# Attention turns: VectorE's copy of the transposed weights issued first in its turn

## The reference, cut to what matters

```python
s_lat = jnp.einsum('bnqhgd,bnkhd->bhgnqk', qb, kb).astype(jnp.float32) * scale
s_lat = jnp.where(valid, s_lat, -jnp.inf)
...
p = jax.nn.softmax(jnp.concatenate([s_lat, s_ctx, s_sink], axis=-1), axis=-1).astype(v.dtype)
out = (jnp.einsum('bhgnqk,bnkhd->bnqhgd', p[..., :nk], vb)
       + jnp.einsum('bhgnqc,bchd->bnqhgd', p[..., nk:nk + nc], vc))
```

## Time and profile before

| | |
|---|---|
| median of 3 runs | 1475.39 us (1473.77 to 1479.74) |
| the profiled execution | 1478.54 us, span of its trace 1476.7 us |
| PE busy | 1359.0 us, 92% of the span |
| DVE busy | 1039.2 us, 70% |
| ACT, POOL busy | 643.8 us, 225.9 us |
| granted TensorE clock, mean | 0.947 of full |
| L995, the copy | 40 times, 526 to 692 ns |
| first pass, in the span | 127.4 to 217.6 us |
| layer 3's pass | 1194.6 to 1230.1 us |

### The profile page before, as it was taken

The page is one execution under the profiler, slowest core; times in us unless marked ns, Lnnn a source line. Parts: engine busy times, 40 slices in busy tenths (PEclk is TensorE's granted clock), DMA queues, the critical chain, the costliest instruction groups (busy, mean ns, idle before and its releaser), DMA issues. The chain is left out here.

```text
span 1476.7 us, 24608 instructions
## 1 busy us (share of the span) xinstructions
PE 1359.0 (92%) x9014; PEld 1177.8 (80%) x9014; DVE 1039.2 (70%) x1803; ACT 643.8 (44%) x1287; POOL 225.9 (15%) x294
## 2 busy tenths in 40 slices
PE   6898999499999999979999999999999978899977
PEld 4576678388888888868896789999899967899857
DVE  0698867889697796988416675766664975755964
ACT  2424761242231423325226654455455465455563
POOL 2030221100000000012102710000210126010324
PEclk7898999699999999989999999999999989899988
DMA  7954124357578575744220155665465533445511
GB/s 279 274 172 156 55 62 143 128 185 268 188 243 284 194 264 179 253 175 143 87 90 25 30 157 171 213 185 185 132 222 171 162 96 107 144 144 170 173 42 44
DMA packets 67799, 236.14 MB, mean 160 GB/s; under 512 B 7296, under 2 KB 12416, under 8 KB 67456
## 3 DMA queue, kind: packets, MB, share of 16 engines
q1 hardware_dynamic: 67712, 234.98, 48.7%
HBM read 233.90 MB, written 1.05 MB: 159 GB/s over the span
## 5 line engine op out<-in xcount | busy, mean ns | idle before, releaser
L768 DVE TENSOR_TENSOR wlo<-raw,whi 128x1024 fp32r<-128x1024 f32 x286 | 361.8, 1267 | 176.4 <-ACT whi L501 171.9
L501 ACT ACTIVATE whi<-raw 128x1024 fp32r<-128x1024 f32 x286 | 301.6, 1055 | 244.3 <-PE ps L1353 232.4
L1351 PE MATMUL ps<-Hh,whi 128*128 128x512 f32 (+1 forms) x848 | 297.2, 351 | 17.3 <-DVE Hl L885 14.2
L1352 PE MATMUL ps<-Hl,whi 128*128 128x512 f32 (+1 forms) x848 | 295.1, 348 | 0.0
L1353 PE MATMUL ps<-Hh,wlo 128*128 128x512 f32 (+1 forms) x848 | 295.0, 348 | 0.0
L1351 PEld LDWEIGHTS ps<-Hh,whi 128*128 128x128 f32 x848 | 162.9, 192 | 41.7 <-issue 14.8
L1351 PE MATMUL ps<-Gh,whi 128*128 128x256 f32 x624 | 180.5, 289 | 4.5 <-DVE Gl L885 3.8
L1352 PEld LDWEIGHTS ps<-Hl,whi 128*128 128x128 f32 x848 | 163.1, 192 | 21.4
L1353 PEld LDWEIGHTS ps<-Hh,wlo 128*128 128x128 f32 x848 | 162.7, 192 | 21.8
L1352 PE MATMUL ps<-Gl,whi 128*128 128x256 f32 x624 | 179.0, 287 | 0.0
L1353 PE MATMUL ps<-Gh,wlo 128*128 128x256 f32 x624 | 178.7, 286 | 0.0
(11 more groups left out here) (212 smaller groups left out, 2110.9 us busy)
## 6 DMA issues: line engine op xcount, KB each, us to landing
raw<-wall SPq DMA_DIRECT2D x286, 512.0 KB, 4.3
aring<-aall SPq DMA_DIRECT2D x144, 512.0 KB, 4.4
AL<-ali SPq DMA_DIRECT2D x14, 192.0 KB, 5.4
X<-xin SPq DMA_DIRECT2D x1, 2048.0 KB, 11.7
BI<-rpb SPq DMA_DIRECT2D x4, 512.0 KB, 16.6
cst<-const SPq DMA_DIRECT2D x1, 1216.0 KB, 11.4
out<-X SPq DMA_DIRECT2D x4, 256.0 KB, 2.5
par<-prm SPq DMA_DIRECT2D x1, 134.5 KB, 2.2
```

The lines of the kernel that those rows point to most:

```text
L501: act.activation(whi[:, slot, :], raw[:, slot, :], ACT.Copy).then_inc(sem("w_hi"), 1)
L768: dve.tensor_tensor(wlo[:, slot, :], raw[:, slot, :], whi[:, slot, :].bitcast(F32), ALU.subtract)\
L1351: pe.matmul(o, a[0], b[0], start=first, stop=False)
L1352: pe.matmul(o, a[0], b[1], start=False, stop=False)
```

## The change

VectorE's copy of head 1's transposed weights of job s-2 is put at the head of its turn, ahead of bias and maximum of job s. Its waits go with it. Nothing is added or removed; no other engine's program changes.

```diff
             def attend(j0, j1):
                 for s in range(j0, j1 + 4):
+                    if j0 <= s - 2 < j1 and not jobs[s - 2].diff:
+
+                        g = s - 2
+                        dve.wait_ge(sem("t_done"), g + 1)
+                        if g >= 2:
+                            dve.wait_ge(sem("pv_done"), g - 1)
+                        dve.tensor_copy(PT[:, g % 2, 1, 0:jobs[g].nk], ps[:, 5, 0:jobs[g].nk]).then_inc(sem("ev_v"), 1)
                     if s < j1:
...
                             dve.scalar_tensor_tensor(e0, e1, st[:, 12:13], e0, ALU.mult, ALU.add)\
                                .then_inc(sem("normed"), 1)
-                    if j0 <= s - 2 < j1 and not jobs[s - 2].diff:
-
-                        g = s - 2
-                        dve.wait_ge(sem("t_done"), g + 1)
-                        if g >= 2:
-                            dve.wait_ge(sem("pv_done"), g - 1)
-                        dve.tensor_copy(PT[:, g % 2, 1, 0:jobs[g].nk], ps[:, 5, 0:jobs[g].nk]).then_inc(sem("ev_v"), 1)
                     if j0 <= s - 4 < j1 and jobs[s - 4].diff:
```

## The result

The changed kernel takes 1485.57 us (median of 4 runs, 1483.78 to 1487.89) against 1475.55 us for the kernel before on the same chip (4 runs, 1473.77 to 1479.74). The ratio is 1.0069, 95% interval 1.0049 to 1.0089: 10.0 us slower, where 8.6 were forecast. The profiled execution took 1486.57 us with a span of 1484.8. The mean granted clock is 0.947 of full in both profiles.

A forecast was written before the change was run, and what follows sets the result against it. It took a VectorE-GpSimd ring to bound layers 3 and 4, and TensorE the first pass. Gated passes 7.0 plus first pass 1.6 gave 8.6 us over 1475.4, so 1484.0 us, with 8 in 10 between 1478.5 and 1488.

The forecast's parts named there:

- The gain: TensorE's 10 waits for the copy, 6.6 us, are all there is to win; six end without moving anything.
- The full turns: Layers 3 and 4: the copy adds 0.44 to each turn, 3.62 to 4.06 us; three distances, 1.32 us a pass.
- the ring: Layers 3 and 4: bias, maximum, reciprocal, GpSimd's widening and gate, product, next bias; this loop sets the turn at 3.62 us.
- The first turns: Layers 3 and 4: the copy waits for the first transposes and delays bias and maximum; first product 2.10 us later.
- The first pass: Stalls of 0.3 us after turns 5, 8 and 11, 0.4 at the end, 0.3 for the fill: 1.6 us.
- the fill: Start of the first pass, not worked out by row: 0.3 us taken, between no loss and 2.1.
- idle until L1501 in each of 24 turns: First pass, sign in the timeline: VectorE's copy waits for TensorE's transposes in every one of 24 turns.
- the clock: Layers 3 and 4: TensorE busy about 3.1 of 4.06 us keeps full clock, so the sum has no term for it.
- The rival made of it: Clock falls to half rate in the longer gaps of layers 3 and 4: +13 us, 1496.5; chance 0.05.
- the softer bound: Layers 3 and 4 less tightly bound, half the loss regained, first pass losing next to nothing: 1479.5 us; chance 0.2.
- the faster case: Every wait for the copy lies on the path that sets the end: -6.6 us, 1468.8; chance 0.04.
- the latency ring in the first pass: Copy, bias, maximum, exponentials and scores follow one another; 24 turns each 0.15 later, 3.6 us more: 1487.5; chance 0.1.

The follow-up runs named there:

- the first pass alone: Against the kernel before, the copy moved to the head of the turn only in the first pass: 1476.76 us against 1477.32, ratio 0.9999.

## Why the prediction was right

**The gain.** That the waits for the copy would go and bring nothing: right. 6.6 us of waits went, the time rose.

**The full turns.** Forecast 4.06, measured 4.08 in each of six distances; the copy holds back by 0.46, not 0.44. The wait for the gate became 1.18, forecast 1.1 to 1.2. That the place sets the price is shown by the kernels with a second copy, and that the ring runs over GpSimd by the kernel that breaks it there.

**The first turns.** The steps gave 2.10 in layer 3, measured 2.05; 2.1 to 2.3 from the end of the first transposes in both passes. Layer 4's number from the pass's start, 2.66, contains clock: between 1407 and 1419 the granted clock was 0.62 to 0.81 before and 0.50 in the changed kernel, whose scores and transposes of turn 3 took 1.65 and 1.33 against 0.93 and 0.85.

**The first pass.** Stalls of 0.3 after turns 5, 8 and 11: 0.26, 0.28 and 0.28; the 0.4 at the end: 0.42. From turn 4 on 1.23 against a forecast of 1.3. The 0.3 taken for the fill can't be told: TensorE waits 0.56 for exponentials ahead of turn 4's scores, which is new, and the 0.33 that it had waited for the copy in turn 3 is gone, but the stretch before turn 4 came out 1.9 us shorter, with a higher granted clock in this profile (the first transposes took 1.09 in place of 1.82), which hides so small a term. Of the forecast's "idle until L1501 in each of 24 turns" 19 of 24 held.

**The step that was wrong** is the clock: "the longer turns here leave it busy for about 3.1 of 4.06, more than that. So the sum has no term for the clock." The full turns do stay at full clock, with 2.82 to 2.90 busy of 4.00. But the row that spoke against a fall, 2.46 of 4.00, is itself from the last turns of the kernel before, and I held the longer full turns against it. Its counterpart in the changed kernel is 2.05. In the first turn after them TensorE has no scores to compute and waits 2.03 us for the last product of the lengthened ring; behind that wait the clock fell in both passes of the profile, 1.85 and 1.15 us. By the prediction's own sign, a granted clock below full in a gated pass after its fill, it is wrong on this point; the time fell in its range all the same, since 3 us of clock fit into it. In the Trainium skill, "TensorE: Matmul & The Clock Gate", section on the HAM clock gate, an idling array is put back to half rate. This trace agrees in the direction: 1.00 to 0.50 behind the wait of 2.03 us. The rival made of it put the fall into the full turns and priced it at 13 us, and neither held.

**The sum.** Gated passes 10.45 in the trace against 7.0, of which 3.0 is the clock in the last turns and the rest, 0.45, the clock in layer 4's first turns and the copy's 0.02. First pass 1.2 against 1.3, its fill apart. With the fill's 1.9 the other way, the passes make 9.7 of the span; the span grew by 8.1. The remaining -1.6 lies outside these passes, where no instruction was moved, and its cause is open; that is as much as gated passes with the same code differ among the profiles (34.0 and 35.6 for layer 3), so the 10.0 of the medians and the 8.1 of the span are one result to within that. That the forecast of 8.6 came within 1.5 of the measured 10.0 is in part luck: the clock added 3.0 that it had at nothing, and the first pass's early stretch and the rest of the kernel gave 3.5 back.

Rivals: the softer bound fell (the distance rose by the whole 0.46), the faster case fell (the gate was waited for still), the latency ring in the first pass fell (1.2 us with the first pass alone) and was found elsewhere.

## What to carry to other kernels

Here an instruction that ran while its engine would have waited for another engine was free in the full turns, and the same instruction inside the ring cost its whole start-to-start time, 0.46 us a turn. So before moving a step earlier, add up the starts around one turn and see whether it lies in the ring or under its cover. The wait that the move removes is worth nothing if the ring sets when the waiting engine runs. Where a ring runs over a third engine, look at that engine's order first: issuing the step that needs only old data ahead of the one that waits for this turn's gave 6.7 us here, and no place tried for VectorE's copy gave any.

## What was not expected of the hardware

In the changed kernel TensorE's granted clock fell from 2.4 to 1.2 GHz in the last turns behind a gap of only 2.03 us, with 2.90 and 2.05 busy in the stretches of 4 us before, at full clock. Over the kernels with the copy at the head of full turns of 4.08 or more it fell in 5 of 8 passes (gap 2.03, in two of them 2.50), and with the copy between maximum and reciprocal in 1 of 2 (longest gap 1.24). The kernel before held full clock in both its last turns with 2.46 busy of 4, and 2.29 in layer 4 (1432 to 1436). The same six transposes then took 1.54 in place of 0.87 us. Under equal waits it fell in one pass and not in another, and 1.95 us of matmuls in the gap left it full in both passes.
